# An encoder layer kernel: the order of work in the attention units rewritten, with the large projections cut in two halves

## What is computed

```
h  = RMSNorm(x)
z  = h @ w_in        # q, k, v, forget, q, k, v, two gates
oA = forgetting attention (8 heads x 64, QK-norm, causal)
oB = differential attention (4 heads, two 64-d q/k maps, 128-d values,
     a = softmax_0 - lam * softmax_1, then RMSNorm of the 128 values)
x1 = x + w_out( sigmoid(gA) * (oA @ w_oa) + sigmoid(gB) * (oB @ w_ob) )
y  = x1 + w_down( silu(a) * b ),  [a|b] = causal conv3( RMSNorm(x1) @ w_up )
```

## Time and profile before

| | us |
|---|---|
| median of three executions | 2154.43 (2153.71 to 2155.83) |
| the profiled execution, device time | 2156.87 |
| its span, from first to last instruction | 2155.3 |
| prologue | 0 to 128.5 |
| units 0 to 3 (kind A) | 128.5 to 650.7: 132.5, 129.7, 129.7 and 130.4 |
| units 4 to 6 (kind B) | 650.7 to 1017.6: 121.8, 122.0 and 123.1 |
| unit 7 (kind B, without projections for a next unit) | 1017.6 to 1102.2: 84.6 |
| merge and feed-forward | 1102.2 to 2155 |
| TensorE busy | 1932.9, 90% of the span |

### The profile page before, as it was taken

One profiled execution on the slowest core, in us unless ns is written; L12 is line 12 of the kernel. 1 busy time (PEld: TensorE's weight loads), 2 busy tenths in 40 slices (PEclk: granted clock), 3 DMA queues, 4 the chain that ended last, 5 costly groups with the idle time before them and its releaser, 6 DMA issues.

```text
span 2155.3 us, 32648 instructions
## 1 busy us (share of the span) xinstructions
PE 1932.9 (90%) x11943; PEld 1793.2 (83%) x11943; DVE 1008.8 (47%) x1958; ACT 787.9 (37%) x1407; POOL 109.2 (5%) x183
## 2 busy tenths in 40 slices
PE   5968898988988788898779999999999999999997
PEld 4857777777777677777669999999999999999987
DVE  4444344443445455445565426554355435544542
ACT  3445445444444445444341123442123112311321
POOL 3100101001000000000000000000000000000011
PEclk8989998999989899898879999999999999999999
DMA  6231413214021221303053321111111111011122
GB/s 201 63 91 30 135 29 101 70 51 130 12 82 51 72 70 51 90 11 102 21 173 122 112 84 37 49 37 43 49 47 36 44 46 49 28 50 49 35 60 68
DMA packets 153955, 144.63 MB, mean 67 GB/s; under 512 B 8009, under 2 KB 134067, under 8 KB 153889
## 3 DMA queue, kind: packets, MB, share of 16 engines
q1 hardware_dynamic: 135296, 78.29, 13.0%
q0 software_dynamic: 18592, 65.46, 9.2%
HBM read 112.61 MB, written 31.11 MB: 67 GB/s over the span
## 4 chain that ended last, share of the span: by engine, by line
PE 56%; DVE 6%; issue 4%; ACT 3%; DMA 2%; DVEq 0%; SPq 0%; POOL 0%; ACTq 0%; POOLq 0%
PE bank L669 30%; PE psS L669 15%; PE psO L669 9%; DMA gate<-gate_scr 1%; PE psT L669 1%; PE psT L860 1%; DMA sqk<-rt_scr 1%; DVE sc L1601 1%; ACT sc L1205 0%; ACT pT_h L1019 0%; DVE o_l L1394 0%; DVE m_a L1693 0%; DVE o_tm L1639 0%; DVE w_l L1394 0%; DVE sc L1618 0%
## 5 line engine op out<-in xcount | busy, mean ns | idle before, releaser
L669 PE MATMUL bank<-xn_hi,w_h 128*128 128x364 f32 (+1 forms) x952 | 338.9, 356 | 14.4 <-DVE xn_lo L1394 11.7
L669 PE MATMUL bank<-xn_lo,w_h 128*128 128x364 f32 (+1 forms) x952 | 326.4, 343 | 0.0
L669 PE MATMUL bank<-xn_hi,w_l 128*128 128x364 f32 (+1 forms) x952 | 325.3, 342 | 0.0
L1019 ACT ACTIVATE w_h<-wraw 128x1024 fp32r<-128x1024 f32 x133 | 139.6, 1050 | 213.6 <-PE psO L669 204.0
L669 PEld LDWEIGHTS bank<-xn_hi,w_h 128*128 128x128 f32 x952 | 192.1, 202 | 28.7 <-issue 21.6
L669 PEld LDWEIGHTS bank<-xn_lo,w_h 128*128 128x128 f32 x952 | 191.3, 201 | 0.0
L669 PEld LDWEIGHTS bank<-xn_hi,w_l 128*128 128x128 f32 x952 | 190.2, 200 | 0.0
L1394 DVE TENSOR_TENSOR w_l<-wraw,w_h 128x1024 fp32r<-128x1024 f32 x133 | 162.3, 1221 | 56.1 <-ACT w_h L1019 55.9
L1333 ACT ACTIVATE ct<-u,vecs 128x1090 f32<-128x1090 f32 x44 | 57.2, 1300 | 327.5 <-DVE u L1752 327.5
L669 PE MATMUL psS<-x_l,w_h 128*128 128x364 f32 (+1 forms) x528 | 173.7, 329 | 0.0
L669 PE MATMUL psS<-x_h,w_l 128*128 128x364 f32 (+1 forms) x528 | 173.6, 329 | 0.0
(11 more groups left out here) (338 smaller groups left out, 4172.0 us busy)
## 6 DMA issues: line engine op xcount, KB each, us to landing
wraw<-in_w_up SPq DMA_DIRECT2D x44, 512.0 KB, 3.9
wraw<-in_w_in SPq DMA_DIRECT2D x41, 512.0 KB, 4.0
gate<-gate_scr POOLq DMA_DIRECT2D x16, 544.0 KB, 4.5
wraw<-in_w_down SPq DMA_DIRECT2D x16, 384.0 KB, 3.4
wraw<-in_w_down SPq DMA_DIRECT2D x16, 320.0 KB, 3.1
x_scr<-xT POOLq DMA_DIRECT2D x8, 544.0 KB, 4.3
cum_s<-c_scr POOLq DMA_DIRECT2D x8, 544.0 KB, 7.4
sqq<-rt_scr SPq DMA_DIRECT2D x16, 272.0 KB, 4.1
```

The costliest lines, as they stand in the source:

```text
L669: return pe.matmul(out, w, x, start=first, stop=last, **kw)
L1019: return act.activation(out, in_, ACT.Copy, **kw)
```

## The change

Four things change. First, the list: the jobs are spread anew over the tiles (V is projected before K; SQ, SK, VT and KT are set apart from one another; a projection job stands between the first chunks of scores), tile 8 comes fourth instead of second, the loads and slots of the weights follow the new order. Second, exponentials become entries of their own (E), placed behind the transposes of the tile before, and ACT's other entries are placed by act_flush. Third, a projection job can stand in the list as HALF (its first 12 matmuls) and again in full (the other 12), with the second transposes of a tile or the next scores between. Fourth, small tiles (0 to 3) use only one half of psT, in turn, and so wait only for the low part two transposes back; ACT's 18 scalings of o_tm in a unit of kind A become one DVE multiplication at OFIN, and its sums of squares in kind B stand one tile later (SQO). SP issues the load of block G1 inside spread_roots instead of behind it.

In kind B the order is the same without the second transposes; C of the next tile stands before the HALF from tile 4 on, behind it for the tiles before. The diff, cut to its core:

```diff
-TILES = [7, 8, 6, 5, 4, 3, 2, 1, 0]
+TILES = [7, 6, 5, 8, 4, 3, 2, 1, 0]
...
+        slots = {"first": ["Q0"], "second": ["Q1"], "third": ["Q2"], (0, 0): ["V0"], (0, 1): ["SQ0"], (1, 0): ["V1"],
+                 (1, 1): ["CS0", "SQ1"], (2, 0): ["V2"], (2, 1): ["SQ2"], (3, 0): ["K0"], (3, 1): ["K1", "SK0"],
+                 (4, 0): ["K2", "SK1"], (4, 1): ["SK2", "VT0"], (5, 0): ["VT1", "VT2"], (5, 1): ["G00"], (6, 0): ["VS0"],
+                 (6, 1): ["G01"], (7, 0): ["G02"], (7, 1): ["KC0"], (8, 0): ["G10", "KC1", "KT0", "KT1", "KT2"], (8, 1): ["G11"],
+                 "end": [ "G12", "OT0", "OT1", "OT2"]}
...
+        slots = {"first": ["G00"], "second": ["G01"], "third": ["G02"], (0, 0): ["G10"], (1, 0): ["G11"], (1, 1): ["CS0"],
+                 (2, 0): ["G12"], "end": ["OT0", "OT1", "OT2"]}
...
+    plan.append(("E", TILES[0]))
+    act_flush()
     scores(1, 0)
...
     for n, i in enumerate(TILES):
         plan.append(("T", i, 0))
         if n:
             plan.append(("AV", TILES[n - 1], maps - 1))
-            flush()
-        if kind == "B" and n + 1 < NT:
+        split_tail = n + 1 < NT and len(KEY_CHUNKS[TILES[n + 1]]) == 3
+        if n + 1 < NT and not split_tail:
+            plan.append(("E", TILES[n + 1]))
+        if kind == "B" and n > 1:
+            plan.append(("SQO", TILES[n - 2]))
+        if kind == "B" and 4 <= n < NT - 1:
             plan.append(("C", TILES[n + 1]))
-        jobs((n, 0))
+        flush()
+        half = slots.get((n, 0), [])[:1]
+        if half and half[0][0] in "VKG" and len(half[0]) == (3 if half[0][0] == "G" else 2):
+            plan.append(("HALF", half[0]))
+        if split_tail:
+            scores(n + 1, 2)
         if kind == "A":
             plan.append(("T", i, 1))
...
+        def turned(self, i, m):
+
+            b = 512 * self.buffer(i, m) if i <= 3 else 0
+            return psT[:, b:1024]
+
+        def turned_after(self, i, m):
+
+            g = self.grp[i, m]
+            before = {n: t for t, n in self.grp.items()}.get(g - 1)
+            return 2 if i <= 3 and before[0] <= 3 else 1
...
-                        pe.wait_ge(S["tl_d"], g - 1)
-                    src = sc[U.turn(i)][m]
+                        pe.wait_ge(S["tl_d"], g - U.turned_after(i, m))
+                    src, out = sc[U.turn(i)][m], U.turned(i, m)
...
-                elif it[0] == "OFIN" and U.kind == "B":
+                elif it[0] == "OFIN" and U.kind == "A":
+                    dve.wait_ge(S["o_d"], U.g0 + 18)
+                    dve.wait_ge(S["rd_d"], U.g0 + 18)
+                    by_head = o_tm[:].rearrange("p t (h d) -> p (t h) d", h=2)
+                    dve.tensor_tensor(by_head, by_head, norm_a[:].rearrange("p t (h a) -> p (t h) a", a=1
+                                                                            ).broadcast_to([P, 2 * NT, DH]),
+                                      ALU.mult).then_inc(S["of_d"], 1)
```

More of the change, by code:

```diff
@@ L70, in unit_plan @@
     if nxt:
[L71 to L75, removed]
-    else:
[L77 to L86, removed]
+        slots = {"first": ["Q0"], "second": ["Q1"], "third": ["Q2"], (0, 0): ["V0"], (0, 1): ["SQ0"], (1, 0): ["V1"],
[4 rows of a table added]
+    else:
+        slots = {"first": ["G00"], "second": ["G01"], "third": ["G02"], (0, 0): ["G10"], (1, 0): ["G11"], (1, 1): ["CS0"],
+                 (2, 0): ["G12"], "end": ["OT0", "OT1", "OT2"]}
+    at_once = {"CS0": [("CB",)]}
+    then = {"CS0": [("VC",)], **({"KT2": [("H", "FIRST")], "VT2": [("ROOT",)]} if nxt else {})}
+    later = {"VS0": [("VB",)], **({"V2": [("VA",)], "VT2": [("RD",)], "G02": [("SCALE",)], "KT2": [("L", "FIRST")]} if nxt else {})}
+    for a, b in WEIGHTS_AFTER[nxt].items():
+        then[a] = then.get(a, []) + [("H", b)]
+        later[a] = later.get(a, []) + [("L", b)]
+    acts, pending = [], []
     plan = [("GS",)]
@@ L104, in unit_plan @@
     scores(0, 0)
+    jobs("first")
     scores(0, 1)
-    jobs("first")
+    jobs("second")
+    plan.append(("E", TILES[0]))
+    act_flush()
     scores(1, 0)
-    jobs("second")
-    flush()
-    scores(1, 1)
-    scores(1, 2)
     if kind == "B":
         plan.append(("C", TILES[0]))
+    flush()
+    jobs("third")
+    scores(1, 1)
     for n, i in enumerate(TILES):
@@ L126, in unit_plan @@
             plan.append(("AV", i, 0))
-            flush()
+        elif split_tail:
+            plan.append(("C", TILES[n + 1]))
+        flush()
+        jobs((n, 0))
+        if nxt and n == 8:
+            plan.append(("SPLIT", 0, 1))
         jobs((n, 1))
+        scores(n + 2, 1)
         if n == 0:
             plan.append(("CA",))
[L131 to L135, removed]
     plan.append(("AV", TILES[-1], maps - 1))
     flush()
+    if kind == "B":
+        plan.append(("SQO", TILES[-2]))
+        plan.append(("SQO", TILES[-1]))
     plan.append(("OFIN",))
@@ L141, in unit_plan @@
     jobs("end")
-    assert not pending
+    assert not pending and not acts
     return plan
-WEIGHTS_AFTER = {True: {"Q0": "K", "K0": "V", "V2": "G0", "G00": "G1"}, False: {"G00": "G1"}}
-BLOCKS = {True: ["Q", "K", "V", "G0", "G1"], False: ["G0", "G1"]}
-SLOT = {"FIRST": 0, "Q": 0, "K": 1, "V": 0, "G0": 0, "G1": 1}
+WEIGHTS_AFTER = {True: {"Q0": "V", "V1": "K", "K2": "G0", "G01": "G1"}, False: {"G00": "G1"}}
+BLOCKS = {True: ["Q", "V", "K", "G0", "G1"], False: ["G0", "G1"]}
+SLOT = {"FIRST": 0, "Q": 0, "V": 1, "K": 0, "G0": 0, "G1": 1}
 def plan_index(plan):
@@ L160, in plan_index @@
                 item[i, c, m] = len(item) + 1
[L161 to L163 removed]
+        elif it[0] == "E":
+            for m in range(2):
+                exp[it[1], m] = len(exp) + 1
         elif it[0] == "T":
@@ L477, in body @@
             load_w(wraw[:], U.block("G0"), gv[U.u][0])
+            last = (wraw[:], U.block("G1"), gv[U.u][1])
             if U.nxt:
-                spread_roots(U.j0 + U.job["SK2"], U.u + 1)
-            load_w(wraw[:], U.block("G1"), gv[U.u][1])
+                spread_roots(U.j0 + U.job["SK2"], U.u + 1, last)
+            else:
+                load_w(*last)
         units(sp, body)
@@ L1625, in body @@
                     high, low = pt[U.buffer(i, m)]
-                    scaled_rest(low[:, 0:n], psT[:, 0:n], P_SCALE if U.kind == "A" else p_scale_b, high[:, 0:n]
+                    scaled_rest(low[:, 0:n], U.turned(i, m)[:, 0:n], P_SCALE if U.kind == "A" else p_scale_b, high[:, 0:n]
                                 ).then_inc(S["tl_d"], 1)
                     if U.kind == "A":
-                        x = U.turn(i)
-                        dve.reciprocal(rden[x][:, m:m + 1], den[x][:, m:m + 1]).then_inc(S["rd_d"], 1)
+                        dve.reciprocal(norm_a[:, i, m:m + 1], den[U.turn(i)][:, m:m + 1]).then_inc(S["rd_d"], 1)
                 elif it[0] == "AV":
```

75 lines of the change are left out of this document (39 added, 36 removed).

## The result

| | before | after |
|---|---|---|
| median | 2154.07 (2149.81 to 2155.83) | 2037.2 (2035.1 to 2040.86) |
| span of the profiled execution | 2155.3 | 2033.6 |
| units 0 to 3 | 132.5, 129.7, 129.7, 130.4 | 112.9, 112.8, 112.6, 112.4 |
| units 4 to 6 | 121.8, 122.0, 123.1 | 107.6, 108.4, 110.8 |
| unit 7 | 84.6 | 73.6 |

The account below looks back on a forecast made before the run. TensorE, busy 90% of the span, was taken as the bound, losing time to waits and half clock in the units. Gains of 58 (kind A), 32 (kind B) and 11 (unit 7), together 101, gave 2053.5 us; range 2022 to 2115.

Parts of the forecast that it names:

- The walk of the waits: New list followed queue by queue with trace durations: TensorE waits of 5.6 us in kind A, 8.7 in kind B.
- S:4:0: Scores of tile 4, waiting for DVE to move the outputs of S:8:2: 2.0 us in kind A, 3.0 in B.
- G00: Projection start behind two short V transposes, needing L:G0: waits of 1.1 us in kind A, 2.2 in kind B.
- the unit's end: End of a kind B unit: output transposes 1.6 us late, copy of G12 another 0.5, together 2.1.
- Unit 7: Last unit, tiles 4 to 0 without projection cover: waits 13 us in place of 25.0, gain 11.
- The halves: Seven projection jobs begun twice in each unit: restarts cost 7 x 0.14 = 1.0 us a unit.
- bare work: Unit length less waiting and half-clock cost before the change: 105.6 us for kind A, 97.6 for kind B.
- The clock: One fall a unit in short work from K2 to G00, perhaps kind B's end: 3 us A, 4 B.
- the second rival: The clock doesn't fall at all, since only idle gaps count: 2025 us, chance 0.12.
- rival one: Clock in the units stays as bad as before, restarts and small waits 1 us more a unit: 2090, chance 0.27.
- no effect: Fourth rival: every wait reappears one entry further on, 2154 us, chance 0.03.
- slower: Third rival: exponential pairs on ACT ahead of the second map's copy leave every tile paying: 2198 us, chance 0.08.

Follow-up runs that it names:

- x_late_lowK: Kernel after the change, with L:K and VC moved behind AV:5:0 (kind A) or C:8 (kind B): 2017.0 us, ratio 0.9353.
- x_y2: x_late_lowK with H:G0 and L:G0 also moved right behind SK2: 2008.6 us, ratio 0.9319.
- x_y3: x_late_lowK with H:G0, L:G0 behind SK2, H:FIRST, L:FIRST behind KT2, and SPLIT of V behind the output transposes: 2002.7 us.
- x_scale_act: Kernel after the change, with kind A's 18 output scalings back on ACT instead of one DVE multiplication: 2082.6 us, ratio 0.9661.
- x_late_exp: Kernel after the change, with each tile's exponentials back right behind its last chunk of scores: 2085.3 us, ratio 0.9671.
- x_whole_psT: Kernel after the change, with all transposes using the whole of psT again, small tiles too: 2042.7 us, ratio 0.9483.
- x_y3_short60: x_y3 with 60 extra transposes of 128 columns ahead of G00 in units 0 to 6: 2066.3 us, ratio 0.9588.

## Why the prediction was right, and where it was off

*The walk of the waits* held, mostly to a few tenths. Kind A, each as walked and as measured: S:4:0 2.0 and 2.0, G00 1.1 and 1.1, KT1 0.9 and 0.7, T:7:1 0.5 and 0.5, SK2 0.3 and 0.3, the output transposes 0.3 and nothing; together 5.6 and 5.7. Kind B: S:4:0 3.0 and 2.9, G00 2.2 and 2.5, the unit's end 2.1 and 1.7 plus 0.4, KT1 0.9 and 0.7; together 8.7, and 9.7 with small ones that I had not seen. Moving the entries to which two of them were laid took those away: with L:K and VC later the wait ahead of S:4:0 fell from 2.0 to nothing in unit 2 and from 2.9 to 0.5 in unit 5 (x_late_lowK), with G0's weights earlier the one ahead of G00 fell from 1.1 to 0.3 and from 2.5 to 1.4 (x_y2). So for these two the causes are shown and not only the sizes. One detail differed: in kind A the trace names ACT's copy v_tm as what G00 waited for, at 1.1 where I had said no wait on v_tm over 1; H:G0 stood ahead of that copy too, and so the same move cures it.

*Unit 7*: forecast 84.6 - 11 = 73.6, measured 73.6. Length less busy time is 15.6, where 13 were walked and 0.6 added for small waits (sc is 8.2 of it in all). The clock gave that back: 0.85 where 0.81 was kept, and 1.6 us less of busy time in spite of the halves. Right in sum by luck: two errors cancel.

*The halves* were priced at 1.0 a unit with a restart cost of 0.14. The bare work with them is 105.1 and 96.7 (x_y3), below the 105.6 and 97.6 that I had worked out without them. So the bare work was put 1.5 and 1.9 too high in all. The restarts cost about half of what I gave them: the first start of a projection group takes 0.25 us instead of 0.17, as before the change, and unit 2 has 21 such starts where it had 15, an estimated 0.5 us a unit. The rest is an error of my estimate of the bare work.

*The clock* is the term that was mis-sized. The cost left after the change was put at 3 us for kind A and 4 for kind B; by busy time it is 106.88 - 105.08 = 1.8 and 98.66 - 96.72 = 1.9. And the place was wrong. I had said that it would fall in G00, behind the run of short work from K2 on. In kind A it did not fall there. It fell at S:4:0, behind the wait of 2.0 for smin. In kind B the place was right in part: in units 5 and 6 the clock fell in G00, behind the wait of 2.5 for w_l, and in unit 4 at S:4:0. The stretches of unit 2 of after around that wait, then from K2's end into G00:

```profile
394.00:398.00 4.00, 2.86 (x23) 2.35 (x21) 2.94 (x6) 2.65 (x4) 0.00 (x0) 1.00 0.00 0
398.00:402.00 4.00, 3.19 (x20) 2.44 (x21) 3.25 (x12) 2.48 (x4) 0.00 (x0) 0.59 0.54 128
402.00:406.00 4.00, 4.00 (x30) 3.02 (x29) 0.60 (x4) 0.93 (x2) 0.00 (x0) 0.99 0.01 3
...
422.00:430.00 8.00, 7.69 (x63) 5.72 (x61) 2.04 (x7) 3.26 (x8) 0.00 (x0) 1.00 0.01 2
430.00:438.00 8.00, 6.82 (x53) 6.13 (x52) 3.73 (x11) 3.58 (x11) 1.43 (x2) 1.00 0.42 128
```

The step that failed is the reading of the earlier trace rows: I took 7 us of short work with 1.9 of waits in it as one cause and never parted the two. The runs part them. After, x_scale_act, x_late_exp, x_late_lowK and x_y3 give TensorE the same matmuls in the same order, with the same short work; slow matmuls in unit 2 are 2, 19, 12, 0 and 0, and follow the waits (5.7, 14.5, 10.6, 3.8 and 4.0 us). They don't follow them closely: x_whole_psT, the same order again, has 7.0 us of waits and none. More short work without more waits (x_y3_short60) brought no fall in G00. So waits decide, with chance in it, and that is nearer to the second rival than to mine. The page "TensorE: Matmul & The Clock Gate" of the Trainium skill, section "HAM oscillation — how this bites in real kernels", lays the fall to idle gaps between blocks of matmuls; its next section, "A second HAM failure mode: psum-queue depth-cycling", adds that small idle times between groups of matmuls bring it too. The traces here agree with both in that every fall in the units of the kernel after stands at a wait or a run of waits, and with the second in that waits of 1.7 to 2.9 us were enough; I had not weighed it. The second rival's time, 2025, was nevertheless too low, because waits of 2 to 3 us were left; once those were taken out too, the clock was full (x_y3).

*The sum.* The profiled execution took 2035.1 against a forecast 2055.9. Of the 20.8, units 0 to 3 gave 13.6 and units 4 to 6 gave 8.1, and prologue and rest took 1 back. The surplus parts in unit 2 into 1.5 of bare work and 1.2 of clock, in unit 5 into 1.9 and 2.1, less 1.0 of waits. The forecast was near because waits carried most of it, and these can be walked. The clock as it is now (rival one, 2090) is refuted by 0.98, and no effect and slower by the result: TensorE's first transposes wait for nothing that ACT's exponentials release in units 2 and 5.

*What the walk can't give*: the worth of a part. Taken out one at a time, the parts cost 67, 45, 48 and 5.5 us, together 166, more than the 117 that the change gains; put in alone, the move of the scalings gives 12. Each wait hides others behind it and can bring the clock down with it.

## What to carry to other kernels

Where several engines walk one list, walk the new list queue by queue with durations from the trace: it gives the waits to a few tenths of a us, and points to the entry to move next (34 us more here from four small moves). Cut long matmul groups where a chain of copies needs covering; here this cost an estimated 0.5 us a unit and its absence 67 us in all. Price an instruction on a busy in-order queue by what it waits for and what stands behind it, not by its duration, and add a price for the clock to TensorE's waits. In unit 2 it was nothing beside 4.0 us of short waits (x_y3), 1.8 beside 5.7 (after), 4.6 beside 14.5 (x_scale_act) and 113.07 - 105.08 = 8.0 beside 16.6 (before).

## What the runs showed of the hardware

The granted clock fell behind waits much shorter than I had thought, and not always. In the traces of all 14 kernels, I took each wait of TensorE of 0.8 us or more between 250 and 1110 us that began at full clock, and looked whether the granted clock fell between its start and 3 us after its end. The last two columns count only waits with no other of 0.5 us or more close by (none that ended in the 5 us before it began or in the 3 us after it ended):

| wait, us | fell | of | alone: fell | of |
|---|---|---|---|---|
| 0.8 to 1.25 | 17 | 138 | 5 | 101 |
| 1.25 to 1.75 | 27 | 70 | 19 | 60 |
| 1.75 to 2.25 | 34 | 50 | 17 | 29 |
| 2.25 to 2.75 | 33 | 40 | 21 | 28 |
| 2.75 to 3.75 | 32 | 39 | 27 | 34 |
| longer | 35 | 35 | 28 | 28 |

The cases are not independent, since units of one kernel repeat one another. But in these counts it is a chance that rises with the wait, not an edge: the wait of 1.96 us ahead of S:4:0 brought 0.59 in unit 2 of the kernel after and left 1.00 in the same place of x_whole_psT:

```profile
398.00:402.00 4.00, 2.29 (x19) 1.78 (x18) 2.94 (x6) 2.08 (x3) 0.00 (x0) 1.00 0.00 0
402.00:406.00 4.00, 3.75 (x31) 3.04 (x32) 2.85 (x11) 2.54 (x5) 0.00 (x0) 1.00 0.52 131
```

So two units that run the same list can differ by some us. In B units of the kernel after, 6, 10 and 23 matmuls were slow with nearly the same waits (9.3, 9.8 and 10.0 us).
